# Compressed keys from strided reads of a turned flow, positions as extra products, low-rank queries behind them

## The chip, the core and the metric

The kernel runs on one core of a Trainium2 chip. A time is the device time of one execution in microseconds (us), and the number that counts is the median of the timed runs. Of TensorE, VectorE, ScalarE, GpSimd and SyncE the profile speaks as PE (PEld for its weight loads), DVE, ACT, POOL and SP.

## The reference, cut to what matters

Two attention layers with large MLPs come first; the change does not touch them. Then one hybrid layer follows. It projects 256 tokens to 1720 columns, and from these it builds two attentions side by side: one with three branches (compressed, selected, window), and one whose queries, keys and values come from low-rank parts. A feed-forward over 16,384 experts ends the kernel. The change lies in the compressed branch and beside it:

```python
n_cmp = (S - CMP_LEN) // CMP_STRIDE + 1          # (256 - 32) // 16 + 1 = 15 blocks of 32 tokens
def compress(t, w1, w2):
    blk = t[:, cmp_idx] + cmp_pos[:, None, :]
    blk = blk.transpose(0, 1, 3, 2, 4).reshape(B, n_cmp, G, CMP_LEN * dk)
    return jax.nn.gelu(blk @ w1) @ w2
kc = compress(k_cmp, cmp_k_w1, cmp_k_w2)
vc = compress(v_cmp, cmp_v_w1, cmp_v_w2)
...
q = (rmsnorm(c_q, q_lora_gain) @ w_uq).reshape(B, S, H, B_QK)
kv = (rmsnorm(c_kv, kv_lora_gain) @ w_ukv).reshape(B, S, H, B_NOPE + B_V)
...
q, k = rmsnorm(q, q_gain), rmsnorm(k, k_gain)
```

Every block is a row of 32 x 64 numbers plus the position table `cmp_pos`, times a matrix of 2048 x 256. There are 15 blocks, two groups g, and two flows a (keys and values).

## The kernel before, in words

Each engine has its own program, written out by hand, and the programs meet at semaphores. The hybrid layer's part is `hybrid_attention` on each engine. It begins when TensorE has multiplied the tokens by `w_in` (`in_product`, PSUM banks 0 to 7); VectorE copies the first 128 tokens to `proj` (L2267), ScalarE the others (L1584 for their squares, L1586).

The *flow* is the pair of column blocks of `proj` that the compression reads. TensorE turns it, 128 columns at a time (L1068). ScalarE copies it out of PSUM as `flow_x0`, even and odd tokens apart (L1593). Four DMAs of SyncE move halves of it to other partitions, as `flow_x`: token parity and channel on the partitions, and for each flow a and group g a row of 128 token pairs (L475). GpSimd adds the positions and writes `blocks`, 16 packed tiles of 30 columns for each flow (L1805). TensorE then multiplies (L1106): for each j of 16, each flow a and each half b of the 256 hidden columns one product with 32 stationary columns and 128 moving ones, into one quarter of bank 3. What comes out goes through a Gelu (L1625), a turn (L1132), a copy (L1627) and the second matrix (L1136), and lands as `kcv`, 30 rows of compressed keys and values. VectorE normalizes and rotates the keys (L2332 to L2344, with a power on GpSimd, L1809). TensorE turns them (L1144), ScalarE copies them to `kcT` (L1643), and TensorE makes the compressed scores (L1150).

Between the turn of the flow and the compression, TensorE keeps itself busy with 26 turns of the identity (L545, `keep_turning`), turns the normalized low-rank parts (L1076), and makes the low-rank queries (L1088, 8 products). ScalarE copies these to `mq` (L1608, L1609) and squares them into `sco` (L1612). VectorE reduces the squares (L2323), multiplies the queries by their gain (L2329) and, after a power on GpSimd (L1739, 16 columns), by their scale (L2346); GpSimd rotates them then (L1815 to L1818).

VectorE takes the compressed scores out of PSUM (L2353 to L2358), puts the mask on the scores of the first two units (L2000), and weighs the compressed output (L2372). After that a loop over 12 units of two heads follows. In each, TensorE turns probabilities (L646), makes scores (L637, L639) and weighs values (L655 to L657); VectorE copies one turned half (L2014), masks (L2000) and accumulates (L2397); ScalarE exponentiates (L1325). The loop turns the low-rank queries two heads at a time, from its second unit on (L1178).

## Time and profile before

| what | value |
|---|---|
| median of 3 timed runs | 1447.3 us (1446.98 to 1447.5) |
| span of the profiled execution, first to last instruction | 1442.5 us |
| mean granted TensorE clock, of full speed | 0.976 |
| PE busy | 1309.3 us, 91% |
| DVE busy | 964.8 us, 67% |
| ACT busy | 546.5 us, 38% |
| POOL busy | 362.6 us, 25% |
| last input product of the hybrid layer ends | 676.8 us |
| loop over the 12 units begins | 711 us |

The profiled execution has no timed value of its own beside its span. The median is 4.8 us above the span, which is what lies before the first and after the last instruction and what one execution differs from another. Busy shares are means over the whole kernel. The change lies in a stretch of some 35 us of it, between the two last lines of the table, so a share of the span says little about it: what counts there is which engine the others wait for.

### The profile page before, as it was taken

How to read it: one execution, taken by the hardware profiler on the slowest of the kernel's cores; microseconds unless marked ns; L12 is line 12 of the kernel's file. 1: busy time of each engine (PE TensorE's matmuls, PEld its weight loads, DVE VectorE, ACT ScalarE, POOL GpSimd, SP SyncE). 2: the span in 40 equal slices, each digit the busy share in tenths (PEclk: the TensorE clock that was granted, in tenths of full speed). 3: DMA queues.
4: the chain of work that ended last, by engine and by line, in shares of the span. 5: the costliest groups of instructions: out<-in, count | busy, mean ns of one | idle time of the engine just before them, and what ended most of it. 6: DMA issues, size and time to landing. Idle time of an engine off the chain costs nothing.

```text
span 1442.5 us, 18328 instructions
## 1 busy us (share of the span) xinstructions
PE 1309.3 (91%) x5884; PEld 899.0 (62%) x5884; DVE 964.8 (67%) x2314; ACT 546.5 (38%) x1129; POOL 362.6 (25%) x378
## 2 busy tenths in 40 slices
PE   8999999999999999999899989878887989788777
PEld 6987888877988888877685744333343535343333
DVE  4687655575566665685864787777767676777755
ACT  4554444444555444455762322222222221222221
POOL 0104000000000000011503455444444443444440
PEclk9999999999999999999999999999998989999999
DMA  9714766545314565565423999999999999999997
GB/s 360 269 59 108 230 188 191 189 160 207 133 40 165 185 190 188 165 223 173 176 90 125 421 420 420 421 421 421 421 421 421 421 422 422 422 421 422 420 421 310
DMA packets 97536, 406.86 MB, mean 282 GB/s; under 512 B 6955, under 2 KB 44524, under 8 KB 60748
## 3 DMA queue, kind: packets, MB, share of 16 engines
q0 software_dynamic: 39552, 276.60, 46.6%
q1 hardware_dynamic: 57932, 129.60, 26.5%
q8 instruction: 29, 0.48, 0.1%
q14 instruction: 23, 0.19, 0.0%
HBM read 404.84 MB, written 1.07 MB: 281 GB/s over the span
## 4 chain that ended last, share of the span: by engine, by line
PE 51%; DMA 22%; issue 13%; DVE 9%; ACT 2%; POOL 2%; DVEq 0%; POOLq 0%; SPq 0%; ACTq 0%
DMA uv_proj<-in_peer_uv,prob 17%; PE ps_up L758 8%; PE ps L699 6%; PE ps L700 6%; PE ps L701 6%; PE ps L870 6%; PE ps_up L760 4%; DMA arena_u<-in_peer_uv,prob 3%; PE ps L940 2%; DMA ring<-in_peer_uv,prob 2%; PE ps_up L699 2%; PE ps_up L701 1%; PE ps_up L700 1%; PE ps_up L840 1%; POOL small L1739 1%
## 5 line engine op out<-in xcount | busy, mean ns | idle before, releaser
L1973 DVE TENSOR_TENSOR w_low<-ring,w_high 128x1024 fp32r<-128x1024 f32 x140 | 165.2, 1221 | 46.1 <-ACT w_high L1268 38.9
L758 PE MATMUL ps_up<-hT_both,w_high 128*128 128x512 f32 x512 | 182.2, 399 | 0.9 <-DVE hT_both L1966 0.9
L1268 ACT ACTIVATE w_high<-ring 128x1024 fp32r<-128x1024 f32 x140 | 140.5, 1052 | 69.9 <-PE ps L701 69.9
L870 PE MATMUL ps<-arena_u,sco 128*128 128x512 f32 x256 | 130.3, 656 | 33.4 <-ACT sco L1522 33.4
L870 PE MATMUL ps<-arena_v,sco 128*128 128x512 f32 x192 | 103.3, 666 | 50.3 <-ACT sco L1522 50.3
L760 PE MATMUL ps_up<-hT_both,w_low 128*128 128x256 f32 x512 | 143.8, 281 | 0.0
L1522 ACT ACTIVATE sco<-const,prob 128x128 f32<-128x128 f32 x256 | 84.7, 391 | 149.8 <-DVE prob L2624 128.5
L1534 ACT ACTIVATE prob<-prob 128x4 f32<-128x4 f32 (+2 forms) x67 | 13.8, 206 | 323.2 <-DVE prob L2614 323.1
L1745 POOL TENSOR_SCALAR small<-small 128x1 f32<-128x1 f32 x8 | 4.3, 535 | 499.3 <-ACT arena_v L1300 499.3
L870 PE MATMUL ps<-ring,sco 128*128 128x512 f32 x256 | 116.5, 604 | 14.3 <-ACT sco L1522 14.3
L2614 DVE CUSTOM_DVE_ANT_0 arena_u<-arena_u,nat 128x1024 f32<-128x1024 f32 x64 | 78.1, 1225 | 67.8 <-DMA arena_u<-in_peer_uv,prob 67.8
L870 PEld LDWEIGHTS ps<-arena_u,sco 128*128 128x128 f32 x256 | 52.9, 210 | 105.3 <-issue 62.0
L1882 POOL DMA_INDIRECT arena_u<-in_peer_uv,prob x64 | 72.9, 1139 | 167.3 <-PE ps L870 100.2
L758 PEld LDWEIGHTS ps_up<-hT_both,w_high 128*128 128x128 f32 x512 | 96.2, 188 | 24.9 <-DVE hT_both L1966 1.3
L870 PEld LDWEIGHTS ps<-arena_v,sco 128*128 128x128 f32 x192 | 36.9, 203 | 108.0 <-ACT sco L1522 71.9
L760 PEld LDWEIGHTS ps_up<-hT_both,w_low 128*128 128x128 f32 x512 | 96.6, 189 | 1.2
L870 PEld LDWEIGHTS ps<-ring,sco 128*128 128x128 f32 x256 | 47.8, 192 | 77.2 <-issue 52.3
L699 PE MATMUL ps<-w_high,act_high 128*128 128x512 f32 x240 | 94.5, 394 | 0.0
L700 PE MATMUL ps<-w_low,act_high 128*128 128x512 f32 x240 | 94.0, 392 | 0.0
L701 PE MATMUL ps<-w_high,act_low 128*128 128x512 f32 x240 | 93.7, 390 | 0.0
L2614 DVE CUSTOM_DVE_ANT_0 arena_v<-arena_v,nat 128x1024 f32<-128x1024 f32 x48 | 58.5, 1223 | 42.6 <-DMA arena_v<-in_peer_uv,prob 42.6
L2614 DVE CUSTOM_DVE_ANT_0 ring<-ring,nat 128x1024 f32<-128x1024 f32 x64 | 78.4, 1225 | 9.1 <-DMA ring<-in_peer_uv,prob 4.7
(480 smaller groups left out, 2884.7 us busy)
## 6 DMA issues: line engine op xcount, KB each, us to landing
ring<-in_w_up SPq DMA_DIRECT2D x32, 1024.0 KB, 5.6
ring<-in_w_down SPq DMA_DIRECT2D x32, 1024.0 KB, 4.9
qkring<-in_qk_a SPq DMA_DIRECT2D x8, 1024.0 KB, 7.1
qkring<-in_qk_b SPq DMA_DIRECT2D x8, 1024.0 KB, 5.0
ring<-in_w_in SPq DMA_DIRECT2D x8, 860.0 KB, 5.4
arena_v<-in_peer_wq SPq DMA_DIRECT2D x5, 1024.0 KB, 9.0
ring<-in_w_out_a SPq DMA_DIRECT2D x4, 1024.0 KB, 16.0
ring<-in_v_b SPq DMA_DIRECT2D x4, 1024.0 KB, 5.9
```

Source lines behind the costliest of these rows:

```text
L699: pe.matmul(dst, a[0], b[0], start=start, stop=False, skip_group_check=True)
L700: pe.matmul(dst, a[0], b[1], start=False, stop=False, skip_group_check=True)
L701: return pe.matmul(dst, a[1], b[0], start=False, stop=stop, skip_group_check=True)
L758: pe.matmul(ps_up[:, 2 * b + fb, :].rearrange("p (a s) -> p a s", a=2), high, hT_both[:, :, c, :], start=(c == 0), stop=False, skip_group_ ...
L760: last = pe.matmul(ps_up[:, 2 * b + fb, S:2 * S], low, hT_high[:, c, :], start=False, stop=(c == NB - 1), skip_group_check=True)
L870: last = pe.matmul(ps[2 * t + n][:, :], diag[:, k % N_DIAG, :], slots[k][:, D + n * HALF:D + (n + 1) * HALF], start=(first and k == 0), st ...
L940: last = pe.matmul(ps[k][:, :], hT[:, c, t * P:(t + 1) * P], ring[:, w_out_slots[c // 2], at:at + HALF], start=(c == 0), stop=(c == NB - 1 ...
L1268: sc.activation(w_split[pair][0][:, part], ring[:, slot, part], ACT.Copy)\
L1522: sc.activation(diag[:, k % N_DIAG, :], ident, ACT.Copy, scale=weight[:, 16 * t + k:16 * t + k + 1])\
L1882: po.indirect_dma_start(slots[k], None, T["peer_uv"], bass.IndirectOffsetOnAxis(ap=expert[:, 16 * t + k:16 * t + k + 1], axis=0))\
L1973: ve.tensor_tensor(w_split[pair][1][:, part], ring[:, slot, part], w_split[pair][0][:, part].bitcast(F32), ALU.subtract)\
L2614: ve.tensor_tensor_reduce(row, row, nat[:, t, :], 1.0, 0.0, ALU.mult, ALU.add, dots[:, k:k + 1])\
```

## The change

`flow_x0`, `blocks`, the four DMAs and GpSimd's additions go. TensorE turns the flow 64 columns at a time, so that both groups land on partitions 0 to 63 (8 turns, L1063 of the new file). ScalarE copies even tokens to partitions 0 to 63 of `flow_x` and odd ones to 64 to 127, straight out of PSUM (L1607, 4 copies). The compression reads its stationary operand from `flow_x` in place: 32 columns, 8 elements apart. Two columns too many come with it, and the copy of the hidden rows skips them. The positions are not added to the blocks; they are multiplied by the same matrix as 64 further products into the same sums, with one column of the table repeated 32 times. The compression moves ahead of the low-rank queries, and its second half behind the turn of the low-rank parts; the identity's turns go. The square of the queries moves behind the compressed keys on ScalarE, and three operations on the queries move behind the compressed keys on VectorE.

```diff
@@ SyncE
-            sp.wait_ge(sem("flow_x0_ready"), count.take("flow_x0_ready"))
-            for g in range(2):
-                for r in range(2):
-                    sp.dma_start(flow_x[64 * r:64 * r + 64, :, g, :], flow_x0[64 * g:64 * g + 64, :, r, :])\
-                        .then_inc(sem("flow_landed"), 16)
@@ TensorE
-                pe.wait_ge(sem("proj_v"), count.take("proj_v", 4))
-                pe.wait_ge(sem("proj_a"), count.take("proj_a", 4))
+                pe.wait_ge(sem("proj_v"), count.take("proj_v", 2))
+                pe.wait_ge(sem("proj_a"), count.take("proj_a", 2))
                 for a in range(2):
-                    for t in range(NT):
-                        last = pe.transpose(ps[0][:, a * S + t * P:a * S + t * P + P],
-                                            proj[:, t, C_KC + a * P:C_KC + a * P + P], ident)
+                    for g in range(2):
+                        for t in range(NT):
+                            at = C_KC + a * P + g * HD
+                            last = pe.transpose(ps[a][0:HD, g * S + t * P:g * S + t * P + P], proj[:, t, at:at + HD], ident)
                 last.then_inc(sem("flow_turned"), 1)
 
-                keep_turning(7, 26)
+                def flow_of(a, j):
+                    return spread(flow_x[:, a, 0, j:], (8, 32))
+
+                def compress(j, src, start=False, stop=False):
+
+                    for a in range(2):
+                        w = ring[:, slots[2 * a + j // 8], :].rearrange("p (c n) -> p c n", c=8)[:, j % 8, :]
+                        for b in range(2):
+                            group = 32 * (2 * a + b)
+                            last = pe.matmul(ps[3][group:group + 32, 0:P], src(a, j), w[:, b * P:(b + 1) * P],
+                                             start=start, stop=stop, skip_group_check=True)
+                    return last
+
+                pe.wait_ge(sem("proj_v"), count.take("proj_v", 2))
+                slots = [slot_of_turn() for _ in range(4)]
+                for j in range(16):
+                    compress(j, lambda a, j: spread(cmp_posT[:, j:j + 1], (0, 32)), start=(j == 0))
+                pe.wait_ge(sem("pool_cleared"), count.take("pool_cleared", 3))
+                pe.wait_ge(sem("flow_x0_ready"), count.take("flow_x0_ready"))
+                for j in range(8):
+                    compress(j, flow_of)
                 pe.wait_ge(sem("lora_ready"), count.take("lora_ready"))
...
+                for j in range(8, 16):
+                    last = compress(j, flow_of, stop=(j == 15))
+                last.then_inc(sem("hidden_done"), 1)
...
+                low_rank_queries(0, 0)
...
+                pe.wait_ge(sem("hidden_ready"), count.take("hidden_ready"))
+                pe.transpose(ps[3][:, P:2 * P], hidden_rows, ident).then_inc(sem("hidden_done"), 1)
+                low_rank_queries(0, 1)
...
+                last.then_inc(sem("kcv_done"), 1)
+                for n in range(2):
+                    low_rank_queries(1, n)
@@ ScalarE
+                sc.wait_ge(sem("flow_turned"), count.take("flow_turned"))
+                for a in range(2):
+                    for r in range(2):
+                        half = slice(r * HD, (r + 1) * HD)
+                        last = sc.activation(flow_x[half, a, :, :],
+                                             ps[a][0:HD, :].rearrange("p (g i r) -> p g i r", g=2, r=2)[:, :, :, r], ACT.Copy)
+                last.then_inc(sem("flow_x0_ready"), 1)
...
-                sc.wait_ge(sem("mq_a"), count.take("mq_a"))
-                sc.activation(flat_sco, mq.rearrange("p t h n -> p (t h n)"), ACT.Square).then_inc(sem("sq_a"), 1)
...
                     sc.activation(v_blocks[32 * n:32 * n + 30, n * HD:(n + 1) * HD], kcv[:, HD:2 * HD], ACT.Copy)
+                sc.wait_ge(sem("mq_a"), count.take("mq_a"))
+                sc.activation(flat_sco, mq.rearrange("p t h n -> p (t h n)"), ACT.Square).then_inc(sem("sq_a"), 1)
@@ GpSimd
-            po.wait_ge(sem("flow_landed"), count.take("flow_landed", 64))
-
-            po.memset(blocks[:, :, :, 30:32], 0.0).then_inc(sem("blocks_ready"), 1)
-            for a in range(2):
-                for g in range(2):
-                    po.tensor_tensor(blocks[:, a, :, 15 * g:15 * g + 15], spread(flow_x[:, a, g, :], (1, 16), (8, 15)),
-                                     spread(cmp_posT, (1, 16), (0, 15)), ALU.add).then_inc(sem("blocks_ready"), 1)
-            rms(0, 16)
             po.wait_ge(sem("kc_ms_ready"), count.take("kc_ms_ready"))
             po.tensor_tensor(rstd[0:30, 0:1], var_eps[0:30, 0:1], neg_half[0:30, 0:1], ALU.pow)\
                 .then_inc(sem("kc_rms_ready"), 1)
+            rms(0, 16)
@@ VectorE
-                queries = mq.rearrange("p t h n -> p (t h) n")
-                low_rank_mean(0, flat_sco)
-                then(ve.tensor_tensor(queries, queries, spread(gain_mq, (0, 16), (1, QK)), ALU.mult))
...
                 ve.tensor_copy(kc_twice[:, HD:P], kc).then_inc(sem("kc_ready"), 1)
-                ve.wait_ge(sem("rms_ready"), count.take("rms_ready"))
-                ve.tensor_tensor(queries, queries, spread(ms_out[:, 0:16], (1, 16), (0, QK)), ALU.mult)\
-                    .then_inc(sem("low_rank_scaled"), 1)
+                queries = mq.rearrange("p t h n -> p (t h) n")
+                ve.wait_ge(sem("sq_a"), count.take("sq_a"))
+                then(ve.tensor_tensor(queries, queries, spread(gain_mq, (0, 16), (1, QK)), ALU.mult))
...
                 ve.tensor_tensor(by_row, by_row, spread(c_peak, (1, 16), (0, 30)), ALU.subtract).then_inc(sem("act_input_ready"), 1)
+                low_rank_mean(0, flat_sco, squared=True)
                 add_bias(0, (0, 1), lambda m: causal)
...
                 add_bias(1, (4, 5), lambda m: causal)
+                ve.wait_ge(sem("rms_ready"), count.take("rms_ready"))
+                ve.tensor_tensor(queries, queries, spread(ms_out[:, 0:16], (1, 16), (0, QK)), ALU.mult)\
+                    .then_inc(sem("low_rank_scaled"), 1)
```

Three places of the order on the engines follow (`arena_u` holds `mq`, `mk` and the compressed scores, `arena_v` holds `flow_x`, `blocks` and `kcv`, `small` the small tables, the positions among them). First TensorE, right behind the last input product, before:

```order
L1068 MATMUL ps<-const,proj 128x128 x4
L545 MATMUL ps_up<-const 128x128 x26
L1076 MATMUL ps<-const,arena_v 128x128 x6
L1088 MATMUL ps_up<-arena_u,relu 128x512 x2
L1088 MATMUL ps_up<-arena_u,relu 128x256 x2
L1088 MATMUL ps_up<-arena_u,relu 128x512 x2
L1088 MATMUL ps_up<-arena_u,relu 128x256 x2
L1106 MATMUL ps<-ring,arena_v 32x128 x64
L1123 MATMUL ps<-const,nat 128x128 x8
L1132 MATMUL ps<-const,arena_v 128x128
L1136 MATMUL ps<-small,arena_v 30x64 x4
```

and with the change:

```order
L1063 MATMUL ps<-const,proj 64x128 x8
L1075 MATMUL ps<-ring,small 32x128 x64
L1075 MATMUL ps<-ring,arena_v 32x128 x32
L1090 MATMUL ps<-const,arena_v 128x128 x6
L1075 MATMUL ps<-ring,arena_v 32x128 x32
L1102 MATMUL ps_up<-arena_u,relu 128x512 x2
L1118 MATMUL ps<-const,arena_v 128x128
L1102 MATMUL ps_up<-arena_u,relu 128x256 x2
L1123 MATMUL ps<-small,arena_v 30x64 x4
L1102 MATMUL ps_up<-arena_u,relu 128x512 x2
L1102 MATMUL ps_up<-arena_u,relu 128x256 x2
```

The low-rank queries (L1088, now L1102) stood ahead of the compression (L1106, now L1075); they now stand behind it, with the turn of the hidden rows and the second matrix (L1118, L1123) between them, and the compression has twice as many products. Second ScalarE, from the copies of the low-rank queries on, before:

```order
L1608 ACTIVATE arena_u<-ps_up 128x512
L1609 ACTIVATE arena_u<-ps_up 128x256
L1608 ACTIVATE arena_u<-ps_up 128x512
L1609 ACTIVATE arena_u<-ps_up 128x256
L1612 ACTIVATE sco<-arena_u 128x1536
L1625 ACT_TABLE_LOAD
L1625 ACTIVATE arena_v<-ps 128x128
L1627 ACTIVATE arena_v<-ps 128x128
L1633 ACTIVATE hT<-ps 128x512 x2
L1637 ACTIVATE hT<-ps 64x512 x2
L1637 ACTIVATE hT<-ps_up 64x512 x2
L1643 ACTIVATE arena_u<-ps 64x30 x2
```

and with the change:

```order
L1632 ACTIVATE arena_u<-ps_up 128x512
L1633 ACTIVATE arena_u<-ps_up 128x256
L1632 ACTIVATE arena_u<-ps_up 128x512
L1633 ACTIVATE arena_u<-ps_up 128x256
L1650 ACTIVATE hT<-ps 128x512 x2
L1654 ACTIVATE hT<-ps 64x512 x2
L1654 ACTIVATE hT<-ps_up 64x512 x2
L1660 ACTIVATE arena_u<-ps 64x30 x2
L1665 ACTIVATE arena_u<-arena_v 30x64 x4
L1667 ACTIVATE sco<-arena_u 128x1536
L1640 ACTIVATE arena_u<-ps_up 128x4x64
```

The square of the queries (L1612, now L1667) has moved behind the heads' copies to `hT` and the copies of the compressed keys and values. Third VectorE, behind the rotation of the heads, before:

```order
L2236 TENSOR_TENSOR nat<-arena_u 128x2x12x8
L2323 TENSOR_REDUCE small<-sco 128x16
L2324 TENSOR_SCALAR small<-small 128x16
L2329 TENSOR_TENSOR arena_u<-arena_u,small 128x1536
L2332 COPY arena_v<-ps 30x128
L2333 ISA arena_v,small<-arena_v 30x64
```

and with the change, from the last copy of the compressed keys on:

```order
L2354 COPY arena_v<-arena_v 30x64
L2357 TENSOR_TENSOR arena_u<-arena_u,small 128x1536
L2363 TENSOR_TENSOR arena_u<-ps,const 128x8x30 x2
L2367 TENSOR_REDUCE small<-arena_u 128x16
L2368 TENSOR_TENSOR arena_u<-arena_u,small 128x16x30
L2337 TENSOR_REDUCE small<-sco 128x16
L2338 TENSOR_SCALAR small<-small 128x16
```

and, further down in VectorE's program, right ahead of the loop:

```order
L2013 ISA peak 128x1
L2013 ISA sco,peak<-ps_up,const 128x256
L2013 ISA peak 128x1
L2388 TENSOR_TENSOR arena_u<-arena_u,small 128x1536
L2027 COPY probT<-ps 128x384
```

The multiplication by the gain (L2329, now L2357) and the reduction (L2323, now L2337) stood ahead of the compressed keys; now they stand on both sides of the compressed scores (L2363 to L2368). The multiplication by the scale (L2388) has moved to the end of the masks, next to the loop's first copy (L2027).

## Rows read from the trace of the kernel before

**Rows 1.** Windows: length, busy PE, PEld, DVE, ACT, POOL (count), clock, DMA share, GB/s
```profile
677.00:712.00 35.00, 28.45 (x278) 21.00 (x280) 28.41 (x69) 24.05 (x57) 23.39 (x25) 1.00 0.52 182
712.00:752.00 40.00, 37.14 (x305) 32.52 (x305) 31.28 (x156) 30.39 (x111) 5.95 (x9) 1.00 0.16 62
```

**Rows 2.** Chain of waits, in order: start us, us, what
```profile
694.00 4.35 POOL small L1739
...
701.45 1.97 PE ps L1150 x16
...
711.07 0.87 PE ps L646 x6
```

**Rows 3.** TensorE timeline: start us, us, instruction, [idle before]
```profile
676.55 0.27 PE L701 MATMUL ps_up<-w_high,hT_both 128*128 128x184 f32 x1
...
679.04 3.00 PE L545 MATMUL ps_up<-const 128*128 128x128 f32 x26
...
683.89 5.43 PE L1088 MATMUL ps_up<-arena_u,relu 128*128 128x512 f32 x16 [0.74 <-ACT relu L1603]
690.38 3.70 PE L1106 MATMUL ps<-ring,arena_v 128*32 128x128 f32 x128 [1.07 <-POOL arena_v L1805]
694.87 1.06 PE L1123 MATMUL ps<-const,nat 128*128 128x128 f32 x8 [0.78 <-PE ps L1106]
...
697.88 1.88 PE L1094 MATMUL ps_up<-arena_u,relu 128*128 128x512 f32 x4
...
717.36 0.60 PE L1178 MATMUL ps_up<-const,arena_u 128*96 128x128 f32 x4
...
690.38 3.43 PEld L1106 LDWEIGHTS ps<-ring,arena_v 128*32 128x32 f32 x128 [1.47 <-POOL arena_v L1805]
```

**Rows 4.** ScalarE timeline, same columns
```profile
679.24 1.09 ACT L1593 ACTIVATE arena_v<-ps 128x256 f32<-128x256 f32 x2
...
689.35 0.60 ACT L1608 ACTIVATE arena_u<-ps_up 128x512 f32<-128x512 f32 x1 [1.71 <-PE ps_up L1088]
689.85 0.38 ACT L1609 ACTIVATE arena_u<-ps_up 128x256 f32<-128x256 f32 x1
690.26 1.49 ACT L1612 ACTIVATE sco<-arena_u 128x1536 f32<-128x1536 f32 x1
...
696.25 1.08 ACT L1633 ACTIVATE hT<-ps 128x512 f32<-128x512 f32 x2
697.64 1.19 ACT L1637 ACTIVATE hT<-ps 64x512 f32<-64x512 f32 x2 [0.31 <-PE ps L1126]
...
701.33 1.05 ACT L1648 ACTIVATE arena_u<-arena_v 30x64 f32<-30x64 f32 x4
```

**Rows 5.** VectorE timeline, same columns
```profile
691.96 1.75 DVE L2323 TENSOR_REDUCE small<-sco 128x16 f32<-128x1536 f32 x1 [0.24 <-ACT sco L1612]
...
693.84 1.75 DVE L2329 TENSOR_TENSOR arena_u<-arena_u,small 128x1536 f32<-128x1536 f32 x1
...
700.45 1.74 DVE L2346 TENSOR_TENSOR arena_u<-arena_u,small 128x1536 f32<-128x1536 f32 x1
703.52 0.72 DVE L2353 TENSOR_TENSOR arena_u<-ps,const 128x240 f32<-128x240 f32 x2 [1.34 <-PE ps L1150]
...
712.04 0.55 DVE L2014 COPY probT<-ps 128x384 f32<-128x384 f32 x1
```

**Rows 6.** GpSimd timeline, same columns
```profile
686.66 3.67 POOL L1805 TENSOR_TENSOR arena_v<-arena_v,small 128x240 f32<-128x240 f32 x4
...
702.26 2.53 POOL L1815 TENSOR_TENSOR arena_u<-arena_u,small 128x256 f32<-128x256 f32 x4 [3.40 <-DVE arena_u L2346]
...
706.89 0.30 POOL L1831 TENSOR_TENSOR arena_u<-proj,small 128x64 f32<-128x64 f32 x1 [0.18 <-POOL arena_u L1818]
```

**Rows 7.** A later window with its clock, and TensorE's timeline there
```profile
850.00:860.00 10.00, 8.81 (x16) 3.55 (x16) 9.46 (x28) 1.48 (x5) 1.34 (x3) 0.83 1.01 421
...
851.19 3.62 PE L870 MATMUL ps<-arena_u,sco 128*128 128x512 f32 x4 [3.17 <-ACT sco L1522]
```

More of the change, by code:

```diff
@@ L1079, in hybrid_attention, with low_rank_queries @@
                         last.then_inc(sem("lora_turned"), 1)
+                for j in range(8, 16):
+                    last = compress(j, flow_of, stop=(j == 15))
+                last.then_inc(sem("hidden_done"), 1)
+                def low_rank_queries(t, n):
+                    a, z = ((0, HALF), (HALF, 768))[n]
+                    for c in range(2):
+                        last = pe.matmul(ps[4 + 2 * t + n][:, 0:z - a], loraT[:, c, t * P:(t + 1) * P],
+                                         w_uq[:, c * 768 + a:c * 768 + z], start=(c == 0), stop=(c == 1))
+                    if n:
+                        last.then_inc(sem("a_side_done"), 1)
+                pe.wait_ge(sem("proj_a"), count.take("proj_a", 2))
                 pe.wait_ge(sem("loraT_ready"), count.take("loraT_ready", 2))
@@ L1084, in hybrid_attention @@
                 landed("qk0")
[L1085 to L1090 removed]
+                low_rank_queries(0, 0)
+                pe.wait_ge(sem("hidden_done"), count.take("hidden_done"))
+                for slot in slots:
+                    pe.sem_inc(sem(f"ring{slot}_used"), 1)
+                turn[0] += 2
+                pe.wait_ge(sem("hidden_ready"), count.take("hidden_ready"))
+                pe.transpose(ps[3][:, P:2 * P], hidden_rows, ident).then_inc(sem("hidden_done"), 1)
+                low_rank_queries(0, 1)
+                pe.wait_ge(sem("hidden_ready"), count.take("hidden_ready"))
+                for a in range(2):
+                    for b in range(2):
+                        last = pe.matmul(ps[2][0:30, a * HD:(a + 1) * HD], hidden[:, a, b, 0:30], cmp_w2[:, a, b, :],
+                                         start=(b == 0), stop=(b == 1))
+                last.then_inc(sem("kcv_done"), 1)
+                for n in range(2):
+                    low_rank_queries(1, n)
                 def key_values(t):
@@ L1130, in hybrid_attention @@
                 turn_heads(range(4))
-                pe.wait_ge(sem("hidden_ready"), count.take("hidden_ready"))
-                pe.transpose(ps[3][:, P:2 * P], hidden_rows, ident).then_inc(sem("hidden_done"), 1)
-                pe.wait_ge(sem("hidden_ready"), count.take("hidden_ready"))
-                for a in range(2):
-                    for b in range(2):
-                        last = pe.matmul(ps[2][0:30, a * HD:(a + 1) * HD], hidden[:, a, b, 0:30], cmp_w2[:, a, b, :],
-                                         start=(b == 0), stop=(b == 1))
-                last.then_inc(sem("kcv_done"), 1)
                 pe.wait_ge(sem("mq_a"), count.take("mq_a"))
@@ L1590, in hybrid_attention @@
                     sc.activation(sq[:, 0, a:z], proj[:, 0, a:z], ACT.Square).then_inc(sem("sq_a"), 1)
-                sc.wait_ge(sem("flow_turned"), count.take("flow_turned"))
-                for a in range(2):
-                    last = sc.activation(flow_x0[:, a, :, :].rearrange("p r i -> p i r"),
-                                         ps[0][:, a * S:(a + 1) * S].rearrange("p (i r) -> p i r", r=2), ACT.Copy)
-                last.then_inc(sem("flow_x0_ready"), 2)
                 sc.wait_ge(sem("proj_a"), count.take("proj_a", 4))
@@ L1603, in hybrid_attention @@
                 sc.activation(loraT[:, 2, :], ps[2][:, 0:S], ACT.Copy).then_inc(sem("loraT_ready"), 1)
+                sc.wait_ge(sem("hidden_done"), count.take("hidden_done"))
+                sc.activation(hidden_rows, ps[3][:, 0:P], ACT.Gelu_apprx_tanh).then_inc(sem("hidden_ready"), 1)
+                sc.wait_ge(sem("hidden_done"), count.take("hidden_done"))
+                sc.activation(spread(hidden[:, 0, 0, :], (32, 4), (15, 2), (1, 15)),
+                              spread(ps[3][:, P:2 * P], (32, 4), (16, 2), (1, 15)), ACT.Copy)\
+                    .then_inc(sem("hidden_ready"), 1)
                 for t in range(NT):
@@ L1794, in _ @@
             po.memset(v_blocks, 0.0)
+            po.memset(av[:, 4464:4472], 0.0)
             po.memset(kcT, 0.0)
```

34 lines of the change are left out of this document (4 added, 30 removed).

## The prediction, made before the change was run

> **What bounds the kernel now.** I read the busy time by windows first. Between 677 and 712 us, from the last input product to the loop over the units, no engine is full: PE is busy 28.5 of 35 us, DVE 28.4, ACT 24.1, POOL 23.4 [rows 1]. So this stretch is bound by a chain that changes engines. In the loop behind it PE is busy 37.1 of 40 us, and DVE idles 8.7 us: a late start there is carried on, not made up for.
>
> The chain of waits shows which chain it is [rows 2]. It runs over GpSimd's power for the low-rank queries (4.35 us from 694.00), then over the compressed scores on TensorE (701.45), and reaches the loop at 711.07. In front of the power stands VectorE's reduction at 691.96 [rows 5]. The timelines tell what each engine does there. TensorE ends the input products at 676.82 (676.55 + 0.27), turns the identity for 3.00 us, makes the low-rank queries from 683.89 on in 5.43 us (so until 689.32), and waits 1.07 us for GpSimd before the compression, 3.70 us from 690.38 [rows 3]. The reader is to see that the compression is late, and that TensorE has some 3 us of idle turning ahead of it: that is room. On VectorE the rows to see are the five at the end [rows 5]: it waits 1.34 us for the compressed scores at 703.52, and from there to the loop's first copy at 712.04 it shows no idle time, 8.52 us of work. The three operations on the queries (1.75 at 691.96, 1.75 at 693.84, 1.74 at 700.45) lie ahead of this, in time in which VectorE waits for others anyway.
>
> **The change, step by step.** I follow it to the loop's first copy on VectorE, 712.04 before, because TensorE's first weighing there waits for that copy.
>
> *TensorE up to the last low-rank query.* From 676.82 on: a wait for its own last product, 0.4 us, an estimate between 0 and the 0.78 us that such a wait with four increments took at 694.87. Eight half-width turns at the pace of the identity's (3.00 us for 26, 0.115 each): 1.0. The position products, as many as the compression before: 3.70. The flow's products: 3.70 + S, where S is what the strided stationary operand costs. Six turns of the low-rank parts at 0.13 (1.06 us for 8): 0.8. The low-rank queries, unchanged: 5.43. A turn and four small products between them, at 0.13 each: 0.65. Sum 15.7 + S, so they end at 692.5 + S, against 689.32 before [rows 3]. The removed identity turns (3.00) only made room for the position products.
>
> ScalarE's four flow copies must be ready when the positions are through, at some 681.9. They can start at 678.4. At the pace of the two strided copies (1.09 for 2) they take 2.2 us, at that of a plain half (0.41 from 689.85 to 690.26) 1.6 [rows 4]. Both are hidden by the positions, and cost what exceeds 3.4 us if they weren't. The four DMAs and GpSimd's additions (3.67 us from 686.66 [rows 6]) were what the compression waited for; leaving them out saves nothing more, because TensorE is now late by itself.
>
> *S, the strided weights.* No row shows a strided weight load, so I bound it. The compression is paced by its loads: 128 take 3.43 of 3.70 us, 0.027 each. The lower end is nothing: the stride is free. The upper end takes a strided load of 32 columns for a contiguous one of 128, 0.115 against 0.029 a pair: 128 x 0.086 = 11.0 us [rows 3]. Two rows lie between. ScalarE writes 256 elements at a stride in 0.545 us, as long as 512 contiguous ones (0.50, from 689.35 to 689.85): double [rows 4]. GpSimd reads this very `flow_x` eight elements apart, 0.92 us for 240 elements, against 0.63 for 256 in its rotation: 1.5 times an element [rows 6]. I take double, the nearest in rate (one element a step, no arithmetic): S = 128 x 0.027 = 3.4 us. The Trainium skill (Advanced Engine Details and Errata, Memory Cachelines) says that SBUF gives its full rate only when successive accesses fall into the same 16-byte line, and a penalty otherwise; by this rule, with every weight on a line of its own, S is above nothing, and without it the sum below would be less by 3.4. No run here shows it for TensorE; ScalarE's row agrees.
>
> *ScalarE up to the square.* Behind the last low-rank query come its two copies (0.50 + 0.41), the heads' copies (1.08 + 1.19 + 1.19, the last a repeat of the 697.64 row), two small copies of the keys at half of four (0.5), the four copies of the values (1.05), and only then the square (1.49): 7.4 us without a wait, since TensorE's turns (8 in 1.06 and 8 more) and key-value product (1.88 [rows 3]) run beside them [rows 4]. So the squares stand at 692.5 + 7.4 = 699.9 + S. Before they stood at 691.8.
>
> *VectorE up to the loop.* Its compressed keys are ready 3 to 6 us earlier than the 700.45 before (an estimate from TensorE's sum), but the multiplication by the gain now waits for the square, since it overwrites what the square reads; and behind it in VectorE's order stand the compressed scores, both masks and the loop. From 699.9 + S it does the gain (1.78 with its gap), the 8.52 us from the scores to the loop, and in between the reduction (1.88, from 691.96 to 693.84) and the scale (1.8): 14.0 us without a wait for another [rows 5]. GpSimd's power (4.35 [rows 2]) lies between reduction and scale, beside two masks, the weights of the compressed probabilities and its output, the larger part of the 8.52 us, and is hidden; with less than 4.35 us there VectorE would wait for the rest. The loop's first copy then starts at 713.9 + S, against 712.04: +1.9 us + S, which is +5.3 us.
>
> What I hold to be nothing: TensorE reaches the compressed scores some us early when S is 0, and no use is made of it, because VectorE takes them only behind the gain. `w_out` and the later loads go out earlier in SyncE's queue; no one waits for them here. GpSimd's rotation, 4.5 us from 702.26 until its next work at 706.89 [rows 6], starts behind the scale at some 713.8 + S and ends at 718.4 + S; TensorE asks for it at 717.36 [rows 3] shifted by the same delay, 719.2 + S or later. It is covered by some 0.9 us.
>
> *The sum.* Against the span of 1442.5 us this is 1447.8. The median is 4.8 above that span, so the forecast is 1452.6 us.
>
> **The rivals.**
>
> *Free stride.* The loads of 32 columns run at the old pace; S = 0. For it speaks that GpSimd's factor on the same data is less than double, and that each load lies beside products of the other three quarters (3.43 us of loads in 3.70 of products [rows 3]), so that a slower one may find cover. Then +1.9 us: 1449.2, 0.13%, which is no difference here: faster or slower by less than 0.2% (2.9 us) can hardly be told from no change.
>
> *The clock falls, or the rotation is late.* TensorE ran into the loop at 711.07 without a long gap; VectorE's delay of 1.9 + S has to appear on TensorE as idle time between the compressed products and the first weighing. At 851.19 an idle time of 3.17 us stands next to a mean granted clock of 0.83 over 10 us, that is 10 x 0.17 / 0.5 = 3.4 us at the lower level of 1.2 GHz [rows 7], with half of that lost: +1.7. In the stretch before the change the clock was 1.00 [rows 1]. Both together with the strided loads: +7.0, 1454.3. A factor of more than two for S ends there too; with one of three S is 6.9 and the time 1456.
>
> *The loop takes it in.* VectorE's delay counts only if the loop's first copy really sets its pace. If TensorE's queue could go on with later units meanwhile, what remains is the compressed branch, whose scores VectorE takes behind the gain at 701.7 instead of 703.52 when S is 0: 1.8 us less. Then 1445.5, and not slower; the wait that the compression had for GpSimd would be won back in part. The point from which it decides is whether the 8.7 us of idle VectorE time in the loop can be moved forward by 2 us; against it speaks that TensorE is busy 37.1 of 40 us and takes the units in a fixed order.
>
> **How the numbers follow.** Strided loads at about double: 0.50. Free stride: 0.27. Clock, rotation or a larger factor: 0.13. The loop takes it in: 0.10. The first and the third are slower by over 0.2%; of the second some 0.04 is, the rest is within it; of the last half is faster. That makes faster 0.05, same 0.28, slower 0.67. The range: below 1448.5 lie the last rival and a third of the free stride, 0.15 together; above 1455.5 lies 0.04. It reaches from 1448.5 to 1455.5.
>
> **What would show it.** Of each step in the changed profile: the position products take 3.7 us and the flow's 7.1 (strided) or 3.7 (free); the last low-rank query ends near 696 or 692.5; ScalarE squares the queries 7 us behind that; VectorE idles some 5 to 7 us in front of the multiplication by the gain, named as waiting for ScalarE's square, and then hardly until the loop; its first copy there starts near 717 or 714; the loop's length stays at what it was. I am wrong if VectorE's wait in front of the gain is short, if it idles again between the gain and the loop, or if the loop is shorter than before.

## The result: slower by 0.3%, near the forecast, and for the most part by another cause

The changed kernel takes 1451.75 us (median of 7 runs, 1449.59 to 1455.44), the kernel before 1447.5 us (7 runs, 1445.14 to 1448.43): 4.25 us more between the medians, or 0.29%. The measured ratio is 1.0035, 95% interval 1.0025 to 1.0045. The ratios here and below are of fast executions; one slow execution of the variant with contiguous weights, 3327.51 us, is left out. The forecast was 1452.6 us. The profiled execution took 1453.32 us, with a span of 1451.5 us.

**Where to begin counting.** In this execution the last input product, which the change does not touch, ends at 680.43 us (680.16 + 0.27), 3.61 us later than the 676.82 of [rows 3]. Two windows ahead of it tell why. The columns are those of [rows 1]. First the kernel before:

```profile
420.00:430.00 10.00, 9.18 (x41) 7.76 (x41) 7.03 (x12) 4.57 (x6) 0.00 (x0) 0.83 0.37 107
638.00:645.00 7.00, 7.00 (x40) 5.97 (x38) 6.66 (x9) 3.27 (x7) 0.15 (x2) 1.00 0.89 342
```

And the changed kernel in the same windows:

```profile
420.00:430.00 10.00, 9.18 (x34) 7.78 (x35) 7.59 (x12) 5.05 (x7) 0.00 (x0) 0.66 0.36 107
638.00:645.00 7.00, 5.85 (x20) 4.77 (x21) 6.72 (x8) 2.95 (x5) 0.74 (x2) 0.76 1.00 387
```

The code there is the same; TensorE's granted clock was lower in this execution. One of the experiments below, a variant of the kernel before, has its last input product at 680.52 with nearly the same clock (0.83 over 420 to 440 us and 0.91 over 640 to 660, as here), and in two variants with the change (turns ahead of the loop, turns in both waits) it ends at 677.5. So these 3.6 us are not the change's, and from here on I count from the end of the last input product.

**TensorE of the changed kernel** (timeline, columns as in [rows 3]):

```profile
680.16 0.27 PE L694 MATMUL ps_up<-w_high,hT_both 128*128 128x184 f32 x1
680.74 1.03 PE L1063 MATMUL ps<-const,proj 128*64 128x128 f32 x8 [0.30 <-PE ps_up L694]
681.70 3.70 PE L1075 MATMUL ps<-ring,small 128*32 128x128 f32 x128
685.22 1.93 PE L1075 MATMUL ps<-ring,arena_v 128*32 128x128 f32 x64
687.88 1.98 PE L1075 MATMUL ps<-ring,arena_v 128*32 128x128 f32 x64
...
693.25 2.85 PE L1102 MATMUL ps_up<-arena_u,relu 128*128 128x512 f32 x8
...
713.87 0.87 PE L639 MATMUL ps<-const,prob 128*128 128x128 f32 x6 [2.64 <-DVE nat L2383]
...
717.20 0.66 PE L648 MATMUL ps_up<-proj,probT 128*128 128x64 f32 x2 [1.28 <-DVE probT L2027]
...
725.40 1.06 PE L1193 MATMUL ps_up<-const,arena_u 128*96 128x128 f32 x4
```

The row of 3.70 us holds the position products (weights from `small`), the two of 1.93 and 1.98 the flow's with their strided weights (`arena_v`): 64 records each, together 3.91 for 128. What the stride costs is settled below, by the variant with contiguous weights. The last low-rank query ends at 696.10, 15.67 us behind the last input product. At the bottom are two waits for VectorE, 2.64 us ahead of the loop and 1.28 us ahead of the first weighing. The second was not there before; the first was 0.78 us:

```profile
711.07 0.87 PE L646 MATMUL ps<-const,prob 128*128 128x128 f32 x6 [0.78 <-DVE nat L2372]
```

The first wait has grown because TensorE comes to it earlier, not because VectorE comes later. TensorE is through with what stands ahead of it 30.80 us behind the last input product (713.87 - 2.64 - 680.43), against 33.47 before (711.07 - 0.78 - 676.82), and goes into the loop at 33.44, against 34.25.

**ScalarE and VectorE.** ScalarE's four flow copies, its last query copies and the square (timeline):

```profile
681.91 1.54 ACT L1607 ACTIVATE arena_v<-ps 64x256 f32<-64x256 f32 x4
...
696.14 0.60 ACT L1632 ACTIVATE arena_u<-ps_up 128x512 f32<-128x512 f32 x1 [2.47 <-PE ps_up L1102]
...
701.77 1.48 ACT L1667 ACTIVATE sco<-arena_u 128x1536 f32<-128x1536 f32 x1
```

VectorE between its compressed keys and the loop (timeline):

```profile
696.76 0.18 DVE L2354 COPY arena_v<-arena_v 30x64 f32<-30x64 f32 x1
703.28 1.76 DVE L2357 TENSOR_TENSOR arena_u<-arena_u,small 128x1536 f32<-128x1536 f32 x1 [6.34 <-ACT sco L1667]
...
714.83 1.75 DVE L2388 TENSOR_TENSOR arena_u<-arena_u,small 128x1536 f32<-128x1536 f32 x1
716.50 0.55 DVE L2027 COPY probT<-ps 128x384 f32<-128x384 f32 x1
```

VectorE waits 6.34 us for ScalarE's square, then works 13.2 us without a gap up to the loop's first copy. That copy starts 36.07 us behind the last input product, against 35.22 before (712.04 - 676.82 [rows 3, 5]): **+0.85 us**. The masks ahead of it end 0.82 us earlier than before (714.83, that is 34.40 against 35.22), and the scale (L2388), which now stands between them and the copy, takes 1.67 us. The chain of waits takes the same way (start, length, what):

```profile
701.77 1.49 ACT sco L1667
703.28 1.77 DVE arena_u L2357
...
716.59 0.48 DVE probT L2027
717.20 0.66 PE ps_up L648 x2
...
729.49 0.22 PE ps_up L649 x2
```

The rest of the loss lies between its last two rows. From the first weighing on the chain is TensorE alone, and a pair of weighing products stands 0.43 to 0.66 us in it at first and 0.22 us from 729.5 on. The windows give the granted clock (the third figure from the end: 0.89, 0.50, ...):

```profile
712.00:716.00 4.00, 2.06 (x14) 1.17 (x14) 3.97 (x13) 2.48 (x11) 0.04 (x1) 0.89 0.00 0
716.00:720.00 4.00, 2.80 (x13) 2.83 (x14) 2.51 (x12) 2.58 (x10) 3.25 (x6) 0.50 0.00 0
720.00:724.00 4.00, 4.00 (x20) 3.02 (x19) 2.67 (x14) 1.47 (x5) 3.58 (x10) 0.50 0.02 4
724.00:728.00 4.00, 4.00 (x20) 3.64 (x21) 2.48 (x9) 2.01 (x8) 2.14 (x4) 0.50 0.00 0
728.00:732.00 4.00, 4.00 (x36) 3.38 (x36) 2.94 (x16) 2.67 (x11) 3.11 (x3) 0.90 0.01 2
```

TensorE runs at 1.2 GHz for about 13.7 us (0.88 + 12 + 0.8), in a place where the whole window had 1.00 before [rows 1], and where it is the bound. The fall begins at about 715.1 us (716 - 0.88), behind the first wait and ahead of the second (715.92 to 717.20). The first low-rank turn comes 44.97 us behind the last input product (725.40 - 680.43), against 40.54 before (717.36 - 676.82 [rows 3]): +4.43, of which 0.85 were there at the first copy and 3.58 came from the clock. The next turn is 5.04 us further where 4.22 stood before (721.58 in the trace of before), another 0.8 in the same stretch.

### The profile page after: what moved, and what is told of

Its sections match the earlier page's. It is cut to its first block, busy times and chain, and to the rows that moved or that the text cites. A ratio compares the mean times of both kernels' runs of the same rounds, so it can differ in the third digit from the quotient of the medians.

```text
span 1451.5 us, 18533 instructions
## 1 busy us (share of the span) xinstructions
PE 1323.6 (91%) x5990; PEld 908.7 (63%) x5990; DVE 962.2 (66%) x2314; ACT 547.5 (38%) x1131; POOL 360.4 (25%) x374
## 4 chain that ended last, share of the span: by engine, by line
PE 52%; DMA 21%; issue 12%; DVE 10%; ACT 3%; POOL 1%; DVEq 0%; POOLq 0%; SPq 0%; ACTq 0%
DMA uv_proj<-in_peer_uv,prob 17%; PE ps_up L751 8%; PE ps L692 7%; PE ps L863 6%; PE ps L693 6%; PE ps L694 6%; PE ps_up L753 4%; DMA arena_u<-in_peer_uv,prob 3%; PE ps L933 2%; PE ps_up L692 2%; PE ps_up L694 1%; PE ps_up L693 1%; PE ps_up L833 1%; PE ps L639 1%; ACT prob L1340 1%
```

## The experiments

Two theories, then. **Clock:** TensorE waits for VectorE around the loop's start, its clock falls, and that is the larger part. **Strided weights or lateness alone:** the prediction's own, by which the clock is an accident of one execution. All ratios are to the kernel before, measured beside it; the last two columns are counted in each trace from the end of its last input product to the loop's first copy on VectorE, and to the first low-rank turn on TensorE. "Waits" are TensorE's ahead of the loop and of the first weighing, "1.2 GHz" is the length of the stretch at granted clock 0.50 that begins around the loop's start (713 to 716 us), worked out from windows as above.

| kernel | ratio (95%) | waits, us | at 1.2 GHz, us | first copy | first turn |
|---|---|---|---|---|---|
| before | 1 | 0.78, - | 0 | 35.22 | 40.54 |
| changed | 1.0035 (1.0025-1.0045) | 2.64, 1.28 | 13.7 | 36.07 | 44.97 |
| changed, again | 1.0033 (1.0020-1.0046) | 2.63, 1.54 | 6.8 | 36.08 | 43.50 |
| turns ahead of the loop | 1.0013 (1.0005-1.0022) | 0.46, 1.60 | 3.4 | 36.08 | 42.71 |
| turns ahead of the weighing | 1.0013 (1.0003-1.0022) | 2.63, - | 3.4 | 36.11 | 42.28 |
| turns in both | 1.0006 (0.9997-1.0014) | 0.45, 0.28 | 0 | 36.08 | 41.17 |
| contiguous weights | 1.0028 (1.0019-1.0037) | 2.64, 1.50 | 6.8 | 36.08 | 43.49 |
| positions behind | 1.0056 (1.0043-1.0069) | 2.64, 0.21 | 10.2 | 38.01 | 46.02 |
| before, VectorE late | 1.0010 (1.0001-1.0018) | 2.62, - | 0 | 37.04 | 42.46 |
| square put back | 1.0012 (1.0001-1.0023) | 2.07, 1.60 | 0 | 35.46 | 40.61 |
| early squares | 0.9989 (0.9980-0.9998) | 0.79, 1.60 | 3.4 | 32.77 | 39.43 |
| split scale, no turns | 0.9973 (0.9962-0.9983) | 0.78, 0.81 | 0 | 31.94 | 37.10 |
| split scale, with turns | 0.9970 (0.9958-0.9982) | 0.78, - | 0 | 31.94 | 37.07 |

**The change again.**

> The changed kernel itself once more, with a new profile. If the 13.65 us at granted clock 0.50 at the loop's start belongs to the change, its profile shows a stretch at 0.50 there again (its length may differ: the contiguous variant of the same timing had 6.83 us) and the ratio is 1.0025 to 1.0045. If the first profile caught an accident, the loop starts at 1.00, its first low-rank turn comes about 41.4 us behind the last input product, and the ratio lies near 1.001, the 0.85 us of VectorE alone.

Measured: 1.0033, and a stretch at 0.50 in the same place, 6.8 us this time. It belongs to the change; its length differed between the two executions that were profiled. The five times of this run spread from 1449.54 to 1452.61 us; only the one of 1449.86 was profiled, so that the spread comes from the clock is not shown.

**Turns ahead of the loop.**

```diff
+                pe.wait_ge(sem("probs_ready"), count.take("probs_ready", 2))
+                keep_turning(0, 20)
                 pe.wait_ge(sem("c_out"), count.take("c_out", 2))
+                count.skip("probs_ready", -2)
```

> The changed kernel with 20 turns of the identity on TensorE, results unused, in the 2.64 us in which it waits for VectorE's weighted rows just ahead of the loop over units; nothing else is changed. The theory that the clock did it (TensorE idles ahead of the loop, its granted clock then shows 0.50 for the first three units, and that is worth about 4.3 us of the loss): the loop's first units run at granted clock 1.00, and the kernel comes back by about 4 us, to 0.999 to 1.002 of the kernel before. If the second gap of 1.28 us, which stays, is enough to let the clock fall, nothing comes back. The theory that strided weights or the late Square alone made it slower: no change, ratio 1.0035, since nothing on their path is touched.

Measured: a ratio in the range that the clock theory gave, but not without a fall: the clock was at 0.50 for 3.4 us. VectorE's first copy did not move (36.08), and still the first turn came 2.26 us earlier than in the first profile of the change (42.71 against 44.97) and the ratio fell by 0.0022, or 3.2 us of 1447. TensorE's timeline shows the second wait left:

```profile
710.98 0.87 PE L639 MATMUL ps<-const,prob 128*128 128x128 f32 x6 [0.46 <-DVE nat L2386]
714.31 0.41 PE L648 MATMUL ps_up<-proj,probT 128*128 128x64 f32 x2 [1.60 <-DVE probT L2030]
```

**Turns in both waits, and ahead of the weighing alone.** The second place is in the loop's first pass:

```diff
                     if u == 2:
                         pe.wait_ge(sem("mkv_a"), count.take("mkv_a"))
+                        keep_turning(6, 10)
```

> The variant with 20 turns ahead of the loop, and 10 more ahead of the first weighing, where TensorE still waited 1.60 us for VectorE's first copy. Clock theory: no stretch at 0.50 at the loop's start; the first low-rank turn comes about 41.4 us behind the last input product (42.7 with the first gap filled alone, 45.0 with none, 40.5 before), ratio about 1.0006. If the clock is not what costs: as with the first gap alone, 42.7 us and ratio 1.0013, or later by the turns.

> The changed kernel with 10 turns of the identity ahead of the first weighing alone; the 2.64 us ahead of the loop stay empty. If the second wait is what lets the clock fall: no stretch at 0.50, first low-rank turn at 41.2 us behind the last input product and ratio 1.0006, as with both waits filled. If the first wait alone is enough: a stretch at 0.50 all the same, the turns run at half speed, turn at 42.7 to 45 us, ratio 1.002 to 1.0035.

Measured with both: first turn at 41.17 (41.4 expected), ratio 1.0006 as expected, and no stretch at 0.50 (windows):

```profile
712.00:716.00 4.00, 3.73 (x34) 3.15 (x33) 3.81 (x14) 2.57 (x13) 2.25 (x4) 1.00 0.01 4
716.00:720.00 4.00, 3.97 (x36) 3.23 (x36) 3.86 (x20) 3.59 (x15) 3.50 (x11) 1.00 0.00 0
```

With the second wait filled alone the clock falls for 3.4 us and the ratio is 1.0013, between the two cases named: in these executions either wait, left empty, was enough for a short fall. This shows that the clock is the larger part. Turns whose results no one uses, put where TensorE waits, take the ratio from 1.0035 to 1.0006. What is left, 0.9 us of 1447, is about VectorE's 0.85 us; its interval (0.9997 to 1.0014) includes none.

**Contiguous weights.**

```diff
-                    return spread(flow_x[:, a, 0, j:], (8, 32))
+                    return spread(flow_x[:, a, 0, j:], (1, 32))
```

> The changed kernel with the flow's products reading 32 neighbouring columns as weights where it reads every eighth; the compressed keys and values are then of wrong tokens, the work is the same in count and shape. The prediction's theory (a strided load costs twice a contiguous one): the 128 flow products fall from 7.1 to 3.7 us and the kernel is 3.4 us faster than the changed one, ratio about 1.001. The theory from the profile after (the stride is free, 64 products took 1.93 and 1.98 us against 3.70 for 128 position products): the products stay at 1.9 to 2.0 us for each half, ratio 1.003 to 1.004.

Measured: 1.0028, an interval that overlaps both showings of the change, and its first copy is at 36.08 as with the stride. TensorE's rows for the flow's halves:

```profile
684.59 1.93 PE L1075 MATMUL ps<-ring,arena_v 128*32 128x128 f32 x64
687.26 1.96 PE L1075 MATMUL ps<-ring,arena_v 128*32 128x128 f32 x64
```

Together 3.89, against 3.91 (1.93 and 1.98) with the stride: it costs at most 0.02 us in all. Yet each load by itself is slower with it. The durations of the 128 flow loads (shortest, median, longest, in ns), with the change and then with contiguous weights:

```profile
L1075 PEld LDWEIGHTS ps<-ring,arena_v x128: 135/138/161, 685.1 to 689.5; 128*32 128x32 f32 x128
L1075 PEld LDWEIGHTS ps<-ring,arena_v x128: 106/110/110, 684.5 to 688.8; 128*32 128x32 f32 x128
```

138 ns against 110. One behind the other, 28 ns more in each of 128 loads would be 3.6 us. They don't stand one behind the other: 128 loads of 110 ns would be 14.1 us, and the kernel before has them within 3.43 us [rows 3], so some four run at a time, and the longer ones find room beside the products. The theory that a strided load adds its own delay falls; that the load is slower holds.

**Positions behind the flow.** The 16 position steps stand behind the first 8 flow steps instead of ahead of them.

> The changed kernel with the 64 position products behind the first half of the flow's products instead of ahead of them, so that TensorE has nothing to do while ScalarE makes the four copies of the flow. Theory that these copies lie hidden behind the positions and that TensorE's chain sets the late Square: TensorE waits about 1.8 us for the copies, the last low-rank query, the Square and the loop's first copy come 1.8 us later (first copy 37.9 us behind the last input product), and the ratio is 1.004 to 1.006. If TensorE's chain does not set the Square: first copy at 36.1 us, ratio as for the change.

Measured: TensorE waits for the copies that lay hidden,

```profile
682.41 1.98 PE L1075 MATMUL ps<-ring,arena_v 128*32 128x128 f32 x64 [1.82 <-ACT arena_v L1607]
```

and the loop's first copy comes at 38.01, 1.94 later. So TensorE's chain to the low-rank queries does set the square, and through it VectorE and the loop; the ratio's further rise has the clock in it (10.2 us at 0.50). The fall begins at some 714.0 us here (granted clock 0.51 over 714 to 716), inside the first wait, which ends at 714.61.

**The kernel before, with VectorE late.** One `tensor_reduce` of 768 elements is made three times:

```diff
+                ve.wait_ge(sem("sq_a"), count.take("sq_a"))
+                count.skip("sq_a", -1)
+                for _ in range(2):
+                    then(ve.tensor_reduce(sq_sum[:, 16:24], mk_sq[:, 0:768].rearrange("p (g d) -> p g d", d=QK), X, ALU.add))
                 low_rank_mean(16, mk_sq[:, 0:768])
```

> The kernel before with the sum of the first tile's key squares made three times instead of once on VectorE (about 1.9 us more), ahead of the weighted rows: TensorE then waits about 2.7 us instead of 0.78 ahead of the loop. The clock theory: the granted clock falls to 0.50 in the loop's first units here too, and the price is 1.9 plus up to 4.3 us, ratio 1.003 to 1.004, without compression or queries being touched. Without the clock: 1.9 us at most, ratio 1.0005 to 1.0013.

Measured: a miss for the clock theory as I had put it. TensorE waited 2.62 us ahead of the loop and its clock stayed at 1.00:

```profile
716.59 0.87 PE L646 MATMUL ps<-const,prob 128*128 128x128 f32 x6 [2.62 <-DVE nat L2376]
```

The price is lateness alone: first copy +1.82, first turn +1.92, ratio 1.0010. So one wait of 2.6 us does not bring the clock down each time. That no second wait follows here does not explain it: in the changed kernel the clock also fell behind 2.63 us with the second wait filled, and in 2.64 us with the positions behind.

**The square put back.** ScalarE's square stands straight behind the query copies again; nothing else of the change is undone.

```diff
                 last.then_inc(sem("mq_a"), 1)
+                sc.wait_ge(sem("mq_a"), count.take("mq_a"))
+                sc.activation(flat_sco, mq.rearrange("p t h n -> p (t h n)"), ACT.Square).then_inc(sem("sq_a"), 1)
...
-                sc.wait_ge(sem("mq_a"), count.take("mq_a"))
-                sc.activation(flat_sco, mq.rearrange("p t h n -> p (t h n)"), ACT.Square).then_inc(sem("sq_a"), 1)
```

> The changed kernel with one part undone: ScalarE's Square of the queries stands straight behind their copies again, ahead of the copies of the turned heads, and not behind the copies of v_blocks. The compressed scores then come about 1.5 us later, but VectorE's gain falls into its wait, so that its masks start 0.9 us earlier than in the changed kernel: first copy at 35.2 us behind the last input product, as before. TensorE's waits ahead of the loop and of the first weighing stay as they are, so by the clock theory a stretch at 0.50 stays too: turn at 42.0 to 44.1 us, ratio 1.001 to 1.0028. If lateness alone made the loss (no clock): ratio 1.000 to 1.0005. If the Square's place does not matter: 1.0033.

Measured: first copy at 35.46, so 0.6 of the 0.85 us was the square's new place. VectorE idles nearly as long as with the change (there 6.34 us for the square), now for the square and then for the compressed scores:

```profile
697.79 1.76 DVE L2357 TENSOR_TENSOR arena_u<-arena_u,small 128x1536 f32<-128x1536 f32 x1 [1.62 <-ACT sco L1636]
703.69 0.72 DVE L2363 TENSOR_TENSOR arena_u<-ps,const 128x240 f32<-128x240 f32 x2 [4.14 <-PE ps L1165]
```

For the clock it is a second miss: the profiled execution shows both waits (2.07 and 1.60 us) and no fall, and its first turn is at 40.61, as before. The ratio of 1.0012 is that of all executions, and they spread: three with a mean clock of 0.976 or 0.977 took 1445.1 to 1445.5 us, three at 0.967 or 0.968 took 1449.2 to 1450.7. That does not show a fall at the loop in some of them: a mean clock lower by 0.009 stands for some 26 us at 0.50 (0.009 x 1447 / 0.5), more than any stretch found there, and of these executions only the one was profiled.

**Early squares.** The square by token tile, the first in ScalarE's wait of 2.47 us, the second ahead of the copies of `v_blocks`; VectorE's gain and reduction by tile behind each.

```diff
+                    if t == 0:
+                        square_queries(t)
...
                 last.then_inc(sem("kcT_ready"), 1)
+                square_queries(1)
```

> The changed kernel with ScalarE's Square of the low-rank queries made by token tile, the first tile's in ScalarE's wait for the second tile's queries and the second's ahead of the copies of v_blocks, and with VectorE's gain and sum of squares done by tile behind each, in its 6.3 us of waiting, ahead of the compressed scores. Theory that the late Square is what holds VectorE: the loop's first copy comes about 2.9 us earlier (33.2 us behind the last input product where it was 36.1). If the clock theory holds too, TensorE's wait ahead of the loop falls from 2.6 to about 1.3 us, the granted clock stays at 1.00, and another 4.3 us come back: ratio 0.996 to 0.998. If the clock falls all the same: ratio about 1.0015. If VectorE's lateness is not what sets the loop's start: ratio 1.0035.

Measured: first copy at 32.77 (33.2 expected), TensorE's wait ahead of the loop 0.79. But the second wait stayed, at 1.60, because VectorE's scale of 1.75 us stands in front of the first copy:

```profile
709.54 1.75 DVE L2397 TENSOR_TENSOR arena_u<-arena_u,small 128x1536 f32<-128x1536 f32 x1
711.21 0.55 DVE L2033 COPY probT<-ps 128x384 f32<-128x384 f32 x1
```

and a short stretch at 0.50 with it: 0.9989, short of the 0.996 to 0.998 of the case without, and better than the 1.0015 of the case with.

**Split scale, with turns and without.** GpSimd's power and VectorE's scale by tile too, the first tile's in VectorE's wait for the second square.

```diff
-            rms(0, 16)
+            for t in range(NT):
+                rms(8 * t, 8)
...
+                    if t == 0:
+                        then(scale_queries(0))
```

> The variant with early squares, and on top: the power and the scale of the queries by token tile too, the first tile's in VectorE's wait of 3.0 us for the second Square, so that 0.9 us less stands ahead of the loop's first copy, and 8 turns of the identity in TensorE's wait ahead of the first weighing. Theory: first copy at 31.9 us behind the last input product (32.8 with early squares alone, 35.2 before), clock 1.00 at the loop's start, first low-rank turn at about 37 us (39.4; 40.5 before) if GpSimd's rotation, which starts only 0.9 us earlier, does not hold it, ratio 0.997 to 0.998. If the rotation holds the low-rank turns: turn at 38.5 us, ratio 0.9985.

> The variant with early squares and split scale without its 8 turns. The first copy stays at 31.9 us behind the last input product. If the waits left (0.8 and some 0.7 us) are too short for the clock to fall: turn at 37.1 us and ratio 0.997 as with the turns. If the clock falls for a short stretch as with early squares alone: turn at about 38.4 us, ratio 0.998.

Measured: first copy 31.94, first turn 37.07 and 37.10, ratios 0.9970 and 0.9973. With waits of 0.78 and 0.81 us the clock stayed at 1.00 without the turns. TensorE's first low-rank turn shows no wait for GpSimd's rotation:

```profile
714.70 0.60 PE L1193 MATMUL ps_up<-const,arena_u 128*96 128x128 f32 x4
```

This beats both kernels: 4.3 us below the kernel before (0.0030 x 1446.7), and 0.65% below the change as it was made (1.0035 against 0.9970).

## Why the prediction was right in the number and wrong in two steps

**TensorE's path: right but for S.** 15.7 us + S were worked out to the last low-rank query; 15.67 were measured, the position products at 3.70 as said, the flow copies 1.54 us and hidden (shown by putting the positions behind).

**S: a step that failed.** "I take double, the nearest in rate (one element a step, no arithmetic): S = 128 x 0.027 = 3.4 us." In the kernel's time S is at most 0.02 us, the lower end that the prediction named and put in the rival "free stride". What was wrong is the overlap. The single load did get slower, by 28 ns, where the prediction added 27; but it was added 128 times in a row, and the loads overlap, as the same rows show [rows 3]. The rival had the mechanism: "a slower one may find cover". That the size of one load came out so near is luck: it was carried over from other engines, and the rows did not say double. ScalarE's strided write of 256 elements (0.545 us) was compared with 512 contiguous ones; against 256 contiguous ones in the same rows (0.41) it is 1.3 times. The rule of the Trainium skill that was cited beside it (Advanced Engine Details and Errata, Memory Cachelines) is a penalty where each access falls on another 16-byte line. These loads take every eighth fp32 element of a row and so another line for each column. The trace agrees for the single load (138 ns against 110) and shows nothing of it in the products' time (1.93 us against 1.93 for the first half). ScalarE's flow copies, which read every second element of PSUM, took 0.385 us each for 256 elements; the plain copy of 256 took 0.38 [rows 4].

**ScalarE and VectorE: right, a little too long.** 7.15 us from the last query to the square's end (7.4 foretold), 6.34 us of waiting in front of the gain (5 to 7), then 13.2 us without a wait (14.0). So +0.85 at the first copy where +1.9 was worked out for S = 0. Two thirds of the 0.8 us on VectorE is one operation on the compressed scores, before and with the change:

```profile
704.97 1.15 DVE L2358 TENSOR_TENSOR arena_u<-arena_u,small 128x480 f32<-128x480 f32 x1
706.52 0.66 DVE L2368 TENSOR_TENSOR arena_u<-arena_u,small 128x480 f32<-128x480 f32 x1
```

GpSimd was at its rotation beside it before and is idle there now; whether that is why, no run shows. GpSimd's power, 2.91 us in place of the 4.35 of [rows 2], was hidden as foretold: it begins at 709.13, and the scale at 714.83 waits for nothing.

**"The loop's length stays at what it was": the other step that failed.** The sum put TensorE's clock at nothing. The rival "the clock falls" came true, with a delay of VectorE of 0.85 us and not of 1.9 + S: TensorE's wait ahead of the loop came from its being early, which the prediction had seen ("some us early when S is 0") and held to be of no use, not to be harmful. The rival's price of 1.7 us was that of a shorter stretch [rows 7]. With 13.7 us at 1.2 GHz it cost 4.4 (3.58 up to the first low-rank turn and 0.8 behind it), with 6.8 us 2.1 (43.50 less 40.54 and 0.86), with 3.4 us some 1 (42.28 less the same 41.40) to 1.3.

**The sum.** Forecast: 1.9 + 3.4 = 5.3. Found in the profiled execution: 0.85 + 4.4 = 5.2. Between the medians of all executions it is 4.25; the second profile of the change, with 6.8 us at 0.50, has 0.86 + 2.1 = 3.0. That the number was right is luck: a cost that isn't in the time (3.4) was near in size to one that I had in a rival at 1.7. "The loop takes it in" did not happen: where the clock held, a delay or gain at the first copy stood at the first turn too, all of it or most (+1.82 and +1.92 with VectorE late, +0.86 and +0.63 with turns in both waits, -3.28 and -3.47 with the scale split).

**What stays open.** When a wait of this length brings the clock down, and for how long. 2.62 us alone did not in the late variant of before, and 2.07 and 1.60 did not in one execution with the square put back. 2.63 us alone did with the second wait filled, 1.60 us behind a wait of 0.46 or 0.79 did, and 2.64 did with the positions behind. Nearly the same two waits were followed by 13.7 us at 0.50 in one execution and by 6.8 in two others. Each of these is one profiled execution of its kernel; the other executions' clocks in this stretch are not known.

## What to carry to other kernels

When the matrix engine is left waiting ahead of a loop that it bounds, look at its granted clock behind the wait as well as at the delay; here the slower clock cost two and a half to five times the delay (2.1 to 4.4 us against 0.85), and turns in the wait (or work moved out of the engine waited for) took it back. An engine that gets done earlier than the one it waits for can lose by it in this way. When an operation is moved behind others on one engine, look at who overwrites or waits for its operand: the square's new place cost 0.6 us at the first copy. VectorE idled some 6 us there with the square in either place, and filling that idle time by tiles was worth more than the whole change had cost. Price a strided read on the engine that does it, and ask whether its longer time stands in a row or beside other work.

## What the runs showed of the hardware

A load of a stationary operand of 32 fp32 columns into TensorE took 138 ns with the columns 32 bytes apart and 110 ns with neighbouring columns (medians of 128). 64 products with such loads took 1.93 to 1.98 us either way, since the loads overlap. TensorE's granted clock fell to 0.50 for 3.4 to 13.7 us at a place where the engine had waited once or twice for 1.3 to 2.6 us; after one wait of 2.62 us in another kernel, and after waits of 2.07 and 1.60 us in one execution of a variant, it did not, and for the same program the length was 13.7 us in one execution and 6.8 in another. Turns of the identity in both waits left it at 1.00.
